# A two-layer decoder trunk on one core: the on-chip tiles placed at other addresses

## What is computed

```python
for layer in range(DEPTH):                       # DEPTH = 2
    if layer % 2 == 0:
        m = pool_nsa_mixer(x, positions, e_w_in[j], ..., e_w_out[j])
    else:
        m = rglru_mixer(x, positions, o_w_in[j], ..., o_w_out[j])
    x = layer_norm(ALPHA * x + m, ln_g[layer, 0], ln_b[layer, 0])
    c = memory_cross_attention(x, mem, x_wq[layer], x_wkv[layer], x_wo[layer])
    x = layer_norm(ALPHA * x + c, ln_g[layer, 1], ln_b[layer, 1])
    f = swiglu(x, f_w_up[layer], f_w_down[layer])     # 1024 -> 2 * 2816 -> 1024
    x = layer_norm(ALPHA * x + f, ln_g[layer, 2], ln_b[layer, 2])
```

## The kernel before

| tiles | start before | mod 512 | mod 64 |
|---|---|---|---|
| x_res, fm_hi, fm_lo, w_raw, w_hi, w_lo, k_mem (k_lo), v_mem (v_lo, silu, gf) | 16512, 32896, 49280, 65664, 73856, 82048, 90240, 98432 | 128 | 0 |
| small tiles (constants, statistics) | 106624 to 111967 | various | 0 or 32 |
| ln_g, ln_b, mem_hi, mem_lo | 111968 to 138591 | 352 | 32 |
| everything at G = 138592: g_hi, g_lo, q_hi, q_lo, pxT_hi, pxT_lo, k_hi, v_hi, kv_tok, qT | G + multiples of 8192 | 352 | 32 |
| ra, ib, h, y_hi, y_lo (recurrent block) | from 138720 | 480 | 32 |

## Time and profile before

### The profile page before, as it was taken

How to read it: one execution, slowest core, us unless ns; L and a number is a source line. 1 busy time by engine, 2 the same in 40 slices (tenths; PEclk the granted TensorE clock), 3 DMA queues, 4 the chain that set the end, 5 groups by cost and what they waited for, 6 DMA issues and landing times.

```text
span 1636.4 us, 21571 instructions
## 1 busy us (share of the span) xinstructions
PE 1565.0 (96%) x7906; PEld 1290.8 (79%) x7906; DVE 554.1 (34%) x924; ACT 632.5 (39%) x1228; POOL 709.5 (43%) x529
## 2 busy tenths in 40 slices
PE   7999999998999999999999988999899999999995
PEld 7879988777888888888887766868787888888884
DVE  2652673444261111100107599643424111101014
ACT  4244553444253333332226367444424333333222
POOL 4552002652365444444447433544144444454443
PEclk9999999999999999999999999999999999999998
DMA  9431001341234333333333423323022333333321
GB/s 228 117 104 53 1 1 39 113 132 52 65 107 142 96 98 91 97 103 92 95 94 106 142 58 90 96 72 91 33 78 73 101 96 91 103 97 96 97 94 61
DMA packets 113602, 147.11 MB, mean 90 GB/s; under 512 B 20374, under 2 KB 69872, under 8 KB 113520
## 3 DMA queue, kind: packets, MB, share of 16 engines
q1 hardware_dynamic: 113200, 145.93, 30.2%
q0 software_dynamic: 320, 0.08, 0.0%
HBM read 143.86 MB, written 2.10 MB: 89 GB/s over the span
## 4 chain that ended last, share of the span: by engine, by line
PE 86%; DVE 6%; ACT 4%; POOL 2%; issue 1%; DMA 0%; DVEq 0%; SPq 0%; ACTq 0%
PE ps L613 75%; PE ps L810 3%; POOL w_lo L562 2%; PE ps L774 2%; PE ps L790 1%; PE ps L873 1%; PE ps L626 1%; PE ps L736 1%; PE ps L841 1%; PE ps L875 1%; ACT px L1264 1%; DVE x_res L1547 1%; DVE tm L1633 0%; DVE a_sq L1629 0%; ACT fm_hi L1024 0%
## 5 line engine op out<-in xcount | busy, mean ns | idle before, releaser
L562 POOL TENSOR_TENSOR w_lo<-w_raw,w_hi 128x512 fp32r<-128x512 f32 (+1 forms) x500 | 680.6, 1369 | 891.0 <-ACT w_hi L1000 888.8
L1000 ACT ACTIVATE w_hi<-w_raw 128x512 fp32r<-128x512 f32 (+1 forms) x500 | 310.3, 627 | 738.0 <-PE ps L613 704.6
L613 PE MATMUL ps<-fm_hi,w_hi 128*128 128x512 f32 (+1 forms) x1096 | 420.2, 383 | 15.1 <-ACT fm_hi L1024 6.3
L613 PE MATMUL ps<-fm_hi,w_lo 128*128 128x512 f32 (+1 forms) x1096 | 418.3, 382 | 0.0
L613 PE MATMUL ps<-fm_lo,w_hi 128*128 128x512 f32 (+1 forms) x1096 | 418.2, 382 | 0.0
L613 PEld LDWEIGHTS ps<-fm_hi,w_hi 128*128 128x128 f32 x1096 | 207.7, 190 | 57.3 <-ACT gelu L1167 7.1
L613 PEld LDWEIGHTS ps<-fm_lo,w_hi 128*128 128x128 f32 x1096 | 207.9, 190 | 39.7 <-issue 0.5
L613 PEld LDWEIGHTS ps<-fm_hi,w_lo 128*128 128x128 f32 x1096 | 207.8, 190 | 39.4
L1744 DVE TENSOR_TENSOR gf<-silu,ps 128x512 f32<-128x512 f32 x44 | 28.3, 683 | 418.6 <-ACT silu L1294 403.2
L1501 DVE SCALAR_TENSOR_TENSOR x_res<-x_res,ps 128x512 f32<-128x512 f32 x48 | 31.4, 684 | 359.6 <-PE ps L613 358.9
L613 PE MATMUL ps<-w_hi,g_hi 128*128 128x512 f32 x352 | 139.0, 395 | 0.0
(11 more groups left out here) (266 smaller groups left out, 1985.0 us busy)
## 6 DMA issues: line engine op xcount, KB each, us to landing
w_raw<-in_f_w_up SPq DMA_DIRECT2D x352, 128.0 KB, 2.1
w_raw<-in_f_w_down SPq DMA_DIRECT2D x88, 256.0 KB, 2.6
w_raw<-in_x_wkv SPq DMA_DIRECT2D x64, 256.0 KB, 3.0
w_raw<-in_o_w_in SPq DMA_DIRECT2D x40, 256.0 KB, 2.7
w_raw<-in_x_wq SPq DMA_DIRECT2D x32, 256.0 KB, 2.6
w_raw<-in_x_wo SPq DMA_DIRECT2D x32, 256.0 KB, 2.6
w_raw<-in_e_w_in SPq DMA_DIRECT2D x24, 256.0 KB, 3.0
w_raw<-in_o_w_out SPq DMA_DIRECT2D x20, 256.0 KB, 2.6
```

The source lines that it names most:

```text
L562: nc.gpsimd.tensor_tensor(w_lo[:, s, :n], w_raw[:, s, :n], w_hi[:, s, :n].bitcast(F32), ALU.subtract).then_inc(w_split, 1)
L613: last = nc.tensor.matmul(outp, lhsT, rhs, start=(clear and k == 0 and n == 0), stop=(k == steps - 1 and n == 2), skip_group_check=True)
L1000: nc.scalar.activation(w_hi[:, s, :n], w_raw[:, s, :n], ACT.Copy).then_inc(w_rounded, 1)
```

## The change

The eight large tiles that stood first now stand behind the small ones, and the first of them starts at a multiple of 512 bytes. The four slots of `w_hi` get 16 columns more each (SKEW), 64 bytes, which nothing reads or writes. No instruction is added, removed or moved on any engine: with the line numbers taken off, the rows of all five engines and their waits are the same. Only addresses differ.

```diff
+SKEW = 16
...
-        x_res, _ = place("x_res", [P, TT, D], F32)
-        fm_hi, _ = place("fm_hi", [P, KT, SEQ], F32R)
-        fm_lo, _ = place("fm_lo", [P, KT, SEQ], F32R)
-        w_raw, _ = place("w_raw", [P, RING, COLS], F32)
-        w_hi, _ = place("w_hi", [P, RING, COLS], F32R)
-        w_lo, _ = place("w_lo", [P, RING, COLS], F32R)
-        k_mem, o_k = place("k_mem", [P, KT, MEM], F32)
-        v_mem, o_v = place("v_mem", [P, MT, D], F32)
         consts, _ = place("consts", [P, C_END], F32)
...
         bias_sel, _ = place("bias_sel", [2 * KT, KT], F32R)
+        cur[0] = (cur[0] + 511) // 512 * 512
+        x_res, _ = place("x_res", [P, TT, D], F32)
+        fm_hi, _ = place("fm_hi", [P, KT, SEQ], F32R)
+        fm_lo, _ = place("fm_lo", [P, KT, SEQ], F32R)
+        w_raw, _ = place("w_raw", [P, RING, COLS], F32)
+        w_hi, _ = place("w_hi", [P, RING, COLS + SKEW], F32R)
+        w_lo, _ = place("w_lo", [P, RING, COLS], F32R)
+        k_mem, o_k = place("k_mem", [P, KT, MEM], F32)
+        v_mem, o_v = place("v_mem", [P, MT, D], F32)
         ln_g, o_ln = place("ln_g", [P, D], F32)
```

## The result

| | before | after |
|---|---|---|
| median | 1641.22 us (4 runs, 1638.18 to 1644.35) | 1653.23 us (4 runs, 1651.13 to 1656.12) |
| ratio | 1 | 1.0078, 95% interval 1.0058 to 1.0099 |
| span of the profiled execution | 1636.4 us | 1648.8 us |

The forecast was 1631.5 us within 1608 to 1652, with 0.14 for slower. The time lies just above the range, on the side I gave least. The spans differ by 12.4 us, like the medians.

The account below looks back on a forecast made before the run. The prediction took PE's distance between matmul starts as the bound. Gains of 9.6 us less 1.4 us lost gave -8.2 us, from 1639.8 to 1631.6, stated as 1631.5 us, range 1608 to 1652.

Parts of the forecast that it names:

- What bounds the kernel: Long products: PE's distance between matmul starts sets the pace, 226.7 or 233.3 ns, no transfer or other engine.
- Rival 1: Matmul distances: addresses do nothing, the two levels come from something else about the tile; 1639.8 us, chance 0.10.
- Is it the address?: 512-column matmuls: either operand starting 32 bytes off a multiple of 64 costs a pass 6.67 ns more.
- A: Follow-up theory: 512-column passes are fast at equal operand starts mod 256, else cost up to 6.67 ns more.
- Part (a): g, y, mem, q, k, v, pxT come to multiples of 64: 9.6 us gained, 7.0 in down products.
- Part (b): 256-column moving operands (memory keys, scores, weighing): aligned they slow to 120 ns, 1.4 us lost.
- Part (c): fm, weights and w_hi slots at new offsets mod 512: likeliest nothing, ends one step of 6.67 ns either way.
- Part (d): ACT, POOL, DVE at other addresses: zero, as POOL's 1379 ns a chunk hides behind PE's 2.7 us.
- Rival 3: fm products: equal offsets mod 512 are good, unequal ones cost; 3080 matmuls slow, +20.5 us, 1658 us, chance 0.14.
- Rival 4: w_hi slots 1 and 3: the unit is 128 bytes, not 64; 11.5 us back, 1643 us, chance 0.06.
- Rival 2: fm products: equal offsets mod 512 make read streams clash, causing the remaining 32 cycles; 20.5 us more gain, 1611, chance 0.20.

Follow-up runs that it names:

- the probe: Kernel of its own without the computation: series of 48 matmuls, one moving and one stationary tile; fp32r, 512 columns: 226.7 ns at equal starts, up to 234.4 otherwise.

## Why the prediction was wrong, point by point

**What bounds the kernel** held: PE's distances between starts, with nothing else in the way. The two levels were read right, and they are set by addresses: in the down product g goes from 233.3 to 226.7 ns when only the upper half is moved. The prediction's 2.4 GHz is one column in 0.417 ns, which its own rows give too, (226.7 - 120.0) / 256. Rival 1 falls.

**"Is it the address?"** is the step that failed. I concluded from two pairs that an operand's own start within 64 bytes counts. With every large operand 32 off a multiple of 64, but at equal distances, the passes take 226.7 ns, and y at a multiple of 64 but 128 bytes from the weights takes 232 to 233: the start counts for nothing, the distance between the two operands mod 256 for up to 7.7 ns. Ein3 fits that, but its blocks at 96 and 608 bytes are also 96 bytes from fm mod 256, so it fits A as well; it excluded the area and nothing more. The row that made me discard A was the cross-attention: 233 ns for three passes of which two have equal starts. That was a group of 12 matmuls. With all starts equal it takes 229.2 ns a matmul instead of 226.7 (changed kernel and each of the four faster ones). That is the start-up of the probe: with the upper half moved its distances are 233, 236, 228, 233 and 231 ns, and then 226 or 227. And the passes of a mixed trio don't keep their prices apart: in slot 1 of wo0 after the change they stand at 236.8, 235.0 and 228.2 ns. A mean over three mixed passes couldn't tell the theories apart, and I used it as if it could.

**Part (a)** had the right size for a wrong reason. The 7.0 us in the down products are there with the upper half moved, since g then stands at the distance 0 from the weights, not since it starts at a multiple of 64. y became a multiple of 64 in the same kernel and gained 2 ns of the 7.6 counted. In the changed kernel the down products gave 1056 x 2.4 = 2.5 us, because the skew put three of four slots away from g as well.

**Part (b)** had the order right: in the probe 256 columns take 120.0 ns at equal starts, else 117.8 to 118.7. Again it is the distance. With the upper half moved the memory keys go from 118.3 to 119.8 ns, the scores from 118.1 to 119.7 and the weighing from 118.2 to 119.5, 1.1 us in all. In the changed kernel the memory keys stay at 118.3, as three of four slots are apart, and fm goes down to 118.7; in sum some 0.2 us were lost where I had 1.4.

**Part (c)** was mis-valued, nothing where +16.7 us (3000 x 4.5 + 768 x 4.2) were due. I wrote that no row showed an aligned operand at another offset, kept both ends at one step, and then took the middle on the strength of the earlier trace rows. The nearest rows, g, y and mem, all stood at unequal distances and all were slow; they spoke for the upper end.

**Part (d)** held: POOL's mean for a chunk of 512 columns is 1372 ns against 1379, and POOL's share of the chain is 2% as before.

**Rival 3** was right, and its price, 1658, was only 5 us too high, in part by luck. It took 512 as the period; with 256 `w_lo` has the distance 0 from fm, so slot 0 stays fast as a whole, 1 in 4 matmuls of fm and not 1 in 6. The other slots cost 5.7 to 6.4 ns more in up0, not 6.67.

By the distance of each pass alone, though, these slots should have cost far less, for a third of their passes, those of `w_lo`, have equal starts. In up0 those take 234.4, 232.5 and 232.0 ns. With the probe's prices slots 1 to 3 come to 231.2, 230.6 and 228.2 ns, where the trace has 233.1, 232.5 and 232.4, and the whole loss on fm to 3768 x 2.4 = 9 us, where it is 16.7. So the distances of the passes explain about half of it, and the rest is there only where equal and unequal passes are mixed. The form counts in that too: in wo0, where the weights are moving, slot 2 at 128 bytes takes 228.8 ns, and slots 1 and 3 take 233.3 and 234.1. Where all three passes of a trio have one distance, the kernels agree with the probe within 0.8 ns: g at 224 takes 233.3 before the change, y at 96 takes 234.3. How a mixed trio gets its price stays open.

Rival 4 falls with the skew alone and with everything 32 bytes off. Rival 2 falls with the probe: at 512 columns no distance is better than 0.

**What hides part of the gain.** The four kernels with equal distances (in two of them y is apart) are ahead by 3.6 to 6.1 us, where I had expected 8 to 10. By the measured distances the upper half moved is worth 7.0 (g) + 0.5 (y) + 0.5 (mem) + 0.1 (weighing) - 1.1 (256 columns) = 7.0 us, and 8.3 with y moved too. Divided at the last three-pass matmul before the attention, at the first one behind it (eout0) and at the last one of dn1, the profiled executions have, in us, and with the granted clock in the attention:

| | up to the attention | attention | eout0 to dn1 | tail | clock in the attention |
|---|---|---|---|---|---|
| before | 150.6 | 115.8 | 1350.2 | 19.8 | 0.97 |
| after | 154.4 | 114.4 | 1360.3 | 19.7 | 0.99 |
| without the skew | 151.6 | 122.0 | 1342.7 | 19.7 | 0.92 |
| upper half moved | 151.6 | 119.1 | 1341.9 | 19.9 | 0.94 |
| y moved too | 154.2 | 119.1 | 1342.2 | 19.9 | 0.94 |
| everything 32 off | 152.7 | 114.4 | 1342.8 | 19.9 | 0.99 |
| skew alone | 152.4 | 118.8 | 1363.9 | 19.8 | 0.94 |
| skew of 128 bytes | 152.8 | 116.1 | 1361.5 | 19.9 | 0.97 |

The long part behaves as counted: 7.4 to 8.3 us less with equal distances. For the changed kernel the agreement of 13.4 us counted with 12.4 measured is one of sums: the stretch up to the attention is 3.8 us longer, where its 312 passes of 512 columns give 1.4, and the long part is 10.1 us longer, where the rest gives 12. The attention moves by up to 7.6 us by itself, and its length follows its clock in all eight executions. Windows over the attention, before and without the skew, all engines:

```profile
150.60:266.40 115.80, 112.16 (x893) 100.45 (x892) 69.88 (x156) 58.39 (x225) 0.96 (x1) 0.97 0.02 7
```

```profile
151.60:273.60 122.00, 118.47 (x893) 106.60 (x892) 69.91 (x156) 58.40 (x225) 0.95 (x1) 0.92 0.02 6
```

The granted clock is 0.97 in the one and 0.92 in the other. In windows of 2 us it is 1.00 in most and 0.50 in unbroken stretches (from 168 to 180 us without the skew). With these two levels, an estimate, that is 2 x 0.03 x 115.8 = 7 us at 0.50 against 2 x 0.08 x 122.0 = 20 us, in a stretch where PE waits again and again. The 12.6 us more at half the clock are an estimate of 6.3 us more, and PE's busy time is 6.3 us longer (118.47 against 112.16).

The runs show the same. Over the 23 runs of the kernel before that stand beside the last three, 0.001 more of mean clock goes with 1.4 us less. The mean clock was 0.9834 in them and 0.9837 in the 11 others, against 0.9827 without the skew, 0.9832 with the upper half moved, 0.9810 with y moved too and 0.9823 with everything 32 off. By that slope, an estimate, the lower clock takes back 1.4, 0.7, 3.5 and 1.6 us, and at the same clock the four kernels would be 7.3, 6.8, 7.1 and 7.5 us ahead, near the 7.0 and 8.3 that the distances give. Why the clock is lower isn't shown. Everything 32 bytes off has 114.4 us in its profiled attention, so equal distances don't force a slow one. Whether the layout has any part in it stays open.

## What to carry to other kernels

When fp32r matmuls of 128 stationary and 512 moving columns follow each other without gaps, put the moving and the stationary tiles at the same remainder mod 256 bytes (226.7 ns in the probe, against 228.9 to 234.4 at other distances), and keep ring slots, rows and column blocks at multiples of 256 apart (227.2 ns in the slots at 0 and 256 from fm, against 234.0 at 128 and 384); here one line that moved a region was worth 0.4%, and a skew of 64 bytes between slots cost 0.8%. Where the tiles themselves start didn't matter (226.7 ns with everything 32 bytes off), and bf16 and plain float32 had 215.8 and 429.2 ns at all five distances. With 256 moving or 64 stationary columns equal starts are not the fastest (120.0 ns against 117.8, 230.0 against 228.5), so measure those. Don't count a mixture pass by pass: one unequal operand in a trio can slow the equal passes beside it, as in up0, where those of `w_lo` take 232.0 to 234.4 ns in slots 1 to 3. When two explanations fit every long stretch of a trace, a short mixed group can't decide between them: a probe of two tiles and 48 matmuls a series does it in one run.

## What the runs showed of the hardware that I had not expected

- In the probe the distance has a sign: stationary 64 bytes past moving costs 233.4 ns, 192 past (64 before) only 228.9. The mixed trios of the kernel don't show it: 192 costs 232.4 in slot 3 of up0 and 233.3 in slot 1 of wo0.
- A series with equal starts can take up to some ten matmuls until it runs at 226.7 ns, so a short group of fast passes isn't a fast group: 12 of them take 229.2 ns each.
- At 256 columns the order is reversed: equal starts 120.0 ns, 64 bytes apart 117.8.
- At equal starts fp32r takes 13.3 ns more than 0.417 ns a column for 256, 384 and 512 moving columns alike (120.0, 173.3 and 226.7 ns). 32 stationary columns at equal starts take 231.7 ns, 5 more than 128, and with 64 equal starts are slower (230.0 ns) than 128 or 192 bytes apart (229.3 and 228.5). The cause is open.
